# Dense part of table v: the low parts of the coefficients on GpSimd, between its gathers, in place of VectorE

## What is computed

```
sv, si = lax.top_k(s, kk)                      # 8 heads, 2 x 128 sub-keys, kk = 16
expert = i1 * PEER_N_KEYS + i2                 # 128 experts for each token
act = jax.nn.gelu(jnp.einsum('tkd,td->tk', u[ex], hx), approximate=False)
return jnp.einsum('tk,tkd->td', gx * act, v[ex])
```

## Time and profile before

| | us |
|---|---|
| median of three runs | 3063.99 |
| the profiled execution | 3068.86 |
| its span, first to last instruction | 3066.9 |
| busy in the span: PE / DVE / ACT / POOL | 2335.1 / 2206.3 / 1266.5 / 1274.6 |
| the dense loop, 2542 to 3048 | 506 |

### The profile page before, as it was taken

The page is one execution under the profiler, slowest core; times in us unless marked ns, Lnnn a source line. Parts: engine busy times, 40 slices in busy tenths (PEclk is TensorE's granted clock), DMA queues, the critical chain, the costliest instruction groups (busy, mean ns, idle before and its releaser), DMA issues.

```text
span 3066.9 us, 38874 instructions
## 1 busy us (share of the span) xinstructions
PE 2335.1 (76%) x15054; PEld 2054.5 (67%) x15054; DVE 2206.3 (72%) x2801; ACT 1266.5 (41%) x2063; POOL 1274.6 (42%) x825
## 2 busy tenths in 40 slices
PE   7899999999999899999999950000233329999997
PEld 2588889988888798999997950000132328888886
DVE  1344446877888873444454599999999988989988
ACT  1233334545555563333334320000597924434433
POOL 0000000245555530000000652588788856767763
PEclk8799999999999999999999985555555569999999
DMA  9887776544454459876554367899999978999996
GB/s 377 342 305 292 291 290 216 181 150 158 165 179 139 151 192 358 334 256 238 199 196 165 136 252 289 300 422 422 422 421 421 421 288 294 362 367 376 357 365 237
DMA packets 152794, 868.47 MB, mean 283 GB/s; under 512 B 18865, under 2 KB 31169, under 8 KB 74705
## 3 DMA queue, kind: packets, MB, share of 16 engines
q1 hardware_dynamic: 68578, 449.03, 39.7%
q0 software_dynamic: 73872, 406.08, 34.2%
q10 hardware_dynamic: 10160, 10.88, 1.0%
HBM read 836.81 MB, written 27.39 MB: 282 GB/s over the span
## 4 chain that ended last, share of the span: by engine, by line
PE 46%; DVE 17%; POOL 13%; DMA 11%; issue 9%; ACT 3%; DVEq 0%; SPq 0%; ACTq 0%; POOLq 0%
PE bank L1789 28%; POOL u_ring L734 13%; PE bank L1775 7%; PE bank L2189 4%; DMA v_got<-in_v_rest,expert 4%; DMA raw<-in_tiles 3%; DVE w_lo L1195 3%; PE bank L1814 2%; DMA u_ring<-in_peer_u,expert 2%; DVE u_ring L1649 2%; DVE peer_g L1690 2%; DMA v_raw<-in_v_dense 2%; DVE conv L1309 1%; DVE c_lo L1703 1%; DVE y_w L1367 1%
## 5 line engine op out<-in xcount | busy, mean ns | idle before, releaser
L1195 DVE TENSOR_TENSOR w_lo<-raw,w_hi 128x1024 fp32r<-128x1024 f32 x450 | 600.0, 1347 | 542.3 <-ACT w_hi L779 536.7
L779 ACT ACTIVATE w_hi<-raw 128x1024 fp32r<-128x1024 f32 x482 | 501.1, 1058 | 639.0 <-PE bank L1789 342.1
L1789 PE MATMUL bank<-h_lo,w_hi 128*128 128x256 f32 x2048 | 592.2, 289 | 12.3 <-DVE h_lo L1241 9.0
L1789 PE MATMUL bank<-h_hi,w_lo 128*128 128x256 f32 x2048 | 581.5, 284 | 0.0
L1789 PE MATMUL bank<-h_hi,w_hi 128*128 128x256 f32 x2048 | 581.5, 284 | 0.0
L734 POOL DMA_INDIRECT u_ring<-in_peer_u,expert x256 | 492.6, 1924 | 199.2 <-DVE act_p L1649 120.4
L1649 DVE CUSTOM_DVE_ANT_0 u_ring<-u_ring,h_t 128x2048 f32<-128x2048 f32 x192 | 435.6, 2289 | 21.1 <-DMA u_ring<-in_peer_u,expert 19.4
L741 POOL DMA_INDIRECT v_got<-in_v_rest,expert x256 | 362.0, 1414 | 179.7 <-DVE peer_g L1690 137.3
L1789 PEld LDWEIGHTS bank<-h_lo,w_hi 128*128 128x128 f32 x2048 | 394.6, 193 | 55.3 <-issue 25.3
L1789 PEld LDWEIGHTS bank<-h_hi,w_lo 128*128 128x128 f32 x2048 | 394.9, 193 | 0.9
L1789 PEld LDWEIGHTS bank<-h_hi,w_hi 128*128 128x128 f32 x2048 | 394.5, 193 | 0.0
(11 more groups left out here) (317 smaller groups left out, 4835.7 us busy)
## 6 DMA issues: line engine op xcount, KB each, us to landing
raw<-in_tiles SPq DMA_DIRECT2D x337, 1024.0 KB, 5.5
v_raw<-in_v_dense SPq DMA_DIRECT2D x128, 660.0 KB, 7.3
s_t<-in_states POOLq DMA_DIRECT2D x8, 512.0 KB, 7.3
y_hi_rows<-y_hi_e POOLq DMA_DIRECT2D x16, 256.0 KB, 2.4
y_lo_rows<-y_lo_e POOLq DMA_DIRECT2D x16, 256.0 KB, 6.3
gate_rows<-gate_buf ACTq DMA_DIRECT2D x8, 512.0 KB, 5.3
y_hi<-y_hi_rows POOLq DMA_DIRECT2D x8, 512.0 KB, 8.0
y_lo<-y_lo_rows POOLq DMA_DIRECT2D x8, 512.0 KB, 4.1
```

What stands on the lines that cost most here:

```text
L779: act.activation(w_hi[:, i % RING], raw[:, slot % SLOTS, (n % 2) * 2 * CH:(n % 2 + 1) * 2 * CH], ACT.Copy) \
L1195: dve.tensor_tensor(w_lo[:, i % RING], raw[:, n // 2 % SLOTS, (n % 2) * 2 * CH:(n % 2 + 1) * 2 * CH], w_hi[:, i % RING].bitcast(F32), ALU. ...
L1789: ins = pe.matmul(spot if x.shape[1] == KT else spot.rearrange("p (s t) -> p s t", s=NS), w[:, col], moving, start=start and k == 0 and m ...
```

## The change

The subtraction that makes `c_lo` goes from VectorE's loop to GpSimd, word for word. It is put between the gathers there: first the gathers up to number 12, then in each step the subtraction of step i and the two gathers 13 + 2i and 14 + 2i. Since it now stands in another engine's order, it brings along its wait for `c_hi` and gets one for TensorE (`dense_done`), which VectorE had from the low part of v ahead of it. No buffer, size or DMA changes.

```diff
@@ -761,8 +761,22 @@
                 gather_v(e)
             pool.wait_ge(pick_turn, 2)
             pool.wait_ge(coef_ready, 3)
-            for e in range(4, NS * SEL):
+            def coef_lo(i):
+                pool.wait_ge(c_hi_done, i + 1)
+                if i >= DENSE:
+                    pool.wait_ge(dense_done, i - DENSE + 1)
+                halves = c_lo[i % DENSE][:].rearrange("p s (h t) -> p s h t", h=2)
+                pool.tensor_tensor(halves, coef_d[:, :, :, i, :],
+                                   c_hi[i % DENSE][:].bitcast(F32).rearrange("p s (h t) -> p s h t", h=2), ALU.subtract) \
+                    .then_inc(c_lo_done, 1)
+
+            added = HALF_B // 2
+            for e in range(4, added + V_RING):
                 gather_v(e)
+            for i in range(N_KEYS):
+                coef_lo(i)
+                for e in range(added + V_RING + 2 * i, min(added + V_RING + 2 * i + 2, NS * SEL)):
+                    gather_v(e)
...
@@ -1733,7 +1740,6 @@
             for i in range(N_KEYS):
                 if i >= 2:
                     dense_lo(i)
-                coef_lo(i)
                 for _ in range(2):
                     if e < NS * SEL:
                         expert_add(e)
```

More of the change, by code:

```diff
@@ L1698, in dense_lo @@
                     .then_inc(v_lo_done, 1)
[L1700 to L1705, removed]
             taken = [0]
```

## The result

The changed kernel takes 3080.27 us, the median of 13 runs (3074.37 to 3107.41), against 3064.51 for the kernel before in as many runs (3056.30 to 3069.58). The ratio is 1.0063, 95% interval 1.0048 to 1.0078. A ratio here is worked out over the fast runs of both kernels, so it is not the quotient of the two medians (1.0051). The changed kernel is slower, as forecast, but by 16 us (15 to 24 by the interval) and not by 83: the time stands where the first rival put it, 3073 to 3088. And it scatters: before, 13 runs lie within 13 us, now within 33. The profiled execution took 3083.74.

What follows compares the result with a forecast made beforehand. TensorE, DVE and the DMA engines were held level before; after the change, POOL's waits set the step. 122 x 4.6 = 561, plus 22 and 5, gave 588 us for 506 (+82): median 3147 us, range 3080 to 3180.

Steps and rivals of the forecast that it cites:

- the first rival: Dense loop: POOL keeps up and DVE's 3.96 us a step bounds; 515 to 530 us, or 3073 to 3088; 14%.
- DVE's 3.75: DVE's step in the dense loop before the change: 3.75 us without gaps, 3.41 after giving away 0.34.
- instruction by instruction: DVE and POOL exclude each other for whole instructions when both read two operands from SBUF.
- The hold-up: POOL's moved subtraction blocks DVE for its span less some 0.15 us: 0.55 a step, making DVE's step 3.96.
- TensorE's 3.73: TensorE's own need per dense-loop step, from 16 steps in 59.69 us; implied 20 of 506 us were waiting.
- the last six steps: Dense-loop steps without gathers, only a subtraction on POOL, running at TensorE's 3.73: 22 us.
- the balance: POOL's step in the dense loop: T = 3.3 + 3 x 2.0 / T, so 4.6 us for 122 steps.
- walk: POOL's instructions traced through DVE's instruction changes: 5.4 us for POOL against DVE's 3.96, so POOL falls behind.
- a subtraction of 1.2 us: Dearer rival: POOL's subtraction takes 1.2 us, T becomes 5.1, time 3207; past 3180 from 0.9 us; 10%.
- Faster: Rival: subtraction in POOL's idle time holds DVE up under 0.34 us, TensorE bounds the dense loop; 3054; 6%.
- TensorE's clock: Rival: TensorE, idle a fifth of each dense-loop step, loses its upper clock level; much slower, no price; 3%.

Runs made afterwards that it cites:

- e1: Changed kernel with GpSimd's subtraction replaced by four memsets of c_lo that read nothing: 3051.02 us, ratio 0.9962 against the kernel before.
- e2: Kernel before with the subtraction on no engine from block 3 on (an old block's low parts used): 3050.60 us, ratio 0.9962.
- e11: Changed kernel with the running sum of gathered rows in two PSUM banks as one buffer, one instruction an addition: 3056.60 us, ratio 0.9977 against before.
- e3: Kernel before with DVE's subtraction kept and GpSimd repeating it into a spare buffer, TensorE waiting for both: 3143.00 us, ratio 1.0255.
- e7: Changed kernel with GpSimd subtracting for only 128 of 256 tokens from block 3 on: 3060.84 us, ratio 0.9992 against the kernel before.
- e4: Changed kernel with DVE subtracting in steps 0 to 23 and GpSimd from step 24: 3088.02 us, ratio 1.0089 against the kernel before.
- e5: Changed kernel unaltered, run and profiled once more: 3085.05 us, ratio 1.0085 against the kernel before; its profiled execution took 3070.28.
- e12: Kernel before, subtraction left on DVE, with the running sum in one PSUM buffer over two banks: 3060.89 us, ratio 0.9993.
- e9: Changed kernel with the running sum in two PSUM banks, each addition in two pieces of 364 columns: 3065.74 us, ratio 1.0006 against before.

## Why the prediction was right or wrong

**Right: that DVE loses.** DVE's 3.75 stands, and e1 and e2 gain 12 us when it is relieved. That two engines exclude each other when both read operands from SBUF was read off and holds: without reading (e1) or with the sum in PSUM (e11) additions are at 0.98 again. That they take turns "instruction by instruction" doesn't hold in e3. The hold-up (forecast 0.55 us, measured 0.41 in the settled step, 0.47 for an addition and 0.53 for a low part of v in the spell) is above the 0.34 given back. The subtraction, forecast at 0.70, has 0.75, with a fixed part of 0.19 as taken.

**Misread: TensorE's 3.73.** The 288 matmuls of the earlier trace rows run in steps that DVE's 3.75 paces, with pauses too short for the chain to show. Left alone, TensorE takes 3.61 a step: in e2, and before from 2862.35 to 2923.82 (17 steps). The loop before then has some 35 us of waiting and not 20. In the sum 3.73 stands for the last six steps alone, so this moves the forecast by under 1 us.

**Wrong: the balance.** The failing step is "an instruction that comes at any moment of a step of T us finds on average ... 2.0 us² / T of waiting", taken three times and for all 122 steps. GpSimd's instructions don't come at any moment. They start when DVE lets them, and their lengths then fix where the next one comes: 0.04, 0.52 and 0.19 us of waiting in the settled step, 0.75 together, against the 1.3 of the sum (3 x 2.0 / 4.6). The prediction had seen such a pattern before the change (0.69 and 0.20 in turn) and named it as what speaks for the first rival.

Its walk was meant to exclude one, but it stops after one round. Worked on by its own terms, the subtraction asks at 10.40 in the second round (the second gather gets going at 9.36 and ends at 10.30, then the gap of "some 0.1"), while the first addition ends at 10.35: missed by 0.05 us, and GpSimd stays behind. That gap was an assumption, as the prediction says; the changed kernel shows 0.02 (2800.75 to 2800.77). With 0.02 the subtraction asks in time, and the same walk closes into an equal step: 3.96 us with the forecast hold-up, 3.82 with the measured terms (hold-up 0.41, subtraction 0.75, gap behind it 0.16), which is the settled step. A walk through a pattern that closes or breaks at 0.05 us can't be made with terms known to 0.1.

In a spell, though, the balance gives the step: 4.58 and 4.61 us against 4.6. The error is how long it holds: none to some 20 steps in the three profiles, where 122 were forecast. 22 steps at 0.76 over the settled 3.82 would be 17 us, 122 would be 93.

**Two slips in the sums** change nothing in this. 3151 less 4.9 is 3146, not 3147. And by its own formula a subtraction of 1.2 us gives T = 5.0 and some 3195, not 5.1 and 3207; 3180 is passed from about 1.1 us on, not from 0.9.

**The first rival** was given 14% and 3073 to 3088; the median is 3080. Its step was put at 3.96, the settled one is 3.82. It left 10 to 25 us for late rows; the loop's 521 less 122 x 3.82 and 22 leaves 33, of which 17 are the spell. What it left out is that the pattern can be lost, which makes the scatter. That its range holds the median is in part luck: its step is 0.14 too long, 17 us in 122 steps, and that stands in for the spell. The stated range, 3080 to 3180, holds 3080.27 by 0.3 us, and only because half of this rival was taken into it.

**Faster** needed a hold-up under 0.34 us. e7 has 0.13 with half the columns and a ratio of 0.9992 (0.9976 to 1.0008): at 0.13 the loss is gone, but no gain can be told from none. **TensorE's clock**: the granted clock is 0.99 over the loop and 1.00 through the spell, 2549 to 2650. Just ahead of it, in 2542 to 2549, it is 0.76 where before it is 1.00: after 2.7 us without work (1.7 before) nine matmuls start 0.37 us apart in place of 0.20, which costs 1.5 us. So the long steps of the spell are not the clock's; in that of e4, 2748 to 2818, it is 0.98.

What stays open: what loses the pattern and what finds it again. In e4 a late row stands at the start of a spell, but the same disturbance in e5 leaves the settled step alone. And why a subtraction that begins inside an addition (e3) holds DVE up for 0.79 and not for 0.41 no run explains.

## What to carry to other kernels

Before work is moved to GpSimd to relieve DVE, lay both timelines over each other: if a span on GpSimd is its shortest value plus the rest of a running DVE instruction, the two exclude each other, and the moved instruction gives part of its span back to DVE as a hold-up (here 0.41 of 0.75 us, 0.13 of 0.47). Then look at where the operands are, not only at which engine does the work: an accumulator in PSUM instead of SBUF turned the same move from a loss of 16 us into a gain of 4. When two engines wait for each other's instruction ends, don't price the waits by an average, and expect runs to scatter; look at several profiles.

## What the runs showed of the hardware

Gathers wait for two-operand DVE instructions as well: in the loop before, 241 of 243 gathers have a span of 0.94 us plus the rest of the DVE instruction that runs, to 0.08 us. They don't hold DVE up (an addition that starts beside one has 0.96 us at 2799.85). With the sum in PSUM a gather doesn't wait for an addition (0.96 us inside one).

The Trainium skill infers that `tensor_tensor` leaves descriptor generation alone (SBUF — State Buffer, Who interferes with whom). These gathers wait for it all the same. They also read their row numbers from SBUF (`expert`), and no run tells whether it is this reading or the descriptors that wait. Its rule that a DVE instruction with at most one SBUF input, outside the 2-port modes, doesn't contend with GpSimd is borne out (e11, 2.06 us for two additions beside GpSimd's subtraction).

An addition of 728 columns costs 0.98 us whether its accumulator is in SBUF or in PSUM, across the border of two banks too (e11, e12). Split into two of 364 it costs 1.11 (e9).

GpSimd's float32 subtraction of 128 x n numbers took 0.47 us for n = 128, 0.75 for 256 and 2.40 for 1024: 0.19 and some 2.2 ns a column.
